# Attention on one core: sinks read as one row per partition ahead of the bias, scores issued behind the first transpositions

## The reference

```python
s = jnp.einsum('bnqhgd,bnkhd->bnhgqk', qb, kb).astype(jnp.float32) * (HEAD_B ** -0.5)
s = jnp.where(valid[None, :, None, None], s + bias[None], NEG_INF)
sink = sinks.astype(jnp.float32).reshape(1, 1, KV_HEADS, Q_PER_KV, 1)
m = jnp.maximum(s.max(-1), sink)
p = jnp.exp(s - m[..., None])
p = p / (p.sum(-1) + jnp.exp(sink - m))[..., None]
return jnp.einsum('bnhgqk,bnkhd->bnqhgd', p, vb.astype(jnp.float32))
```

## Time and profile before

| | us |
|---|---|
| median of 3 runs | 1780.65 (1779.14 to 1781.78) |
| the profiled execution, its own time | 1773.95 |
| its span, from first to last instruction | 1772.0 |
| attention stage (`at_` tiles), from the trace | 335.5 to about 467 |

### The profile page before, as it was taken

The page is one execution under the profiler, slowest core; times in us unless marked ns, Lnnn a source line. Parts: engine busy times, 40 slices in busy tenths (PEclk is TensorE's granted clock), DMA queues, the critical chain, the costliest instruction groups (busy, mean ns, idle before and its releaser), DMA issues. The chain is left out here.

```text
span 1772.0 us, 30746 instructions
## 1 busy us (share of the span) xinstructions
PE 1500.0 (85%) x12413; PEld 925.7 (52%) x12414; DVE 621.9 (35%) x1000; ACT 363.0 (20%) x797; POOL 200.3 (11%) x262
## 2 busy tenths in 40 slices
PE   7999999676787888537995799999499399999968
PEld 4666666455687777313442344444388244444433
DVE  1122460187134343562335111111578511111117
ACT  1232110166222322210001111111122111111111
POOL 3000000000222311320000101110500011111030
PEclk8999999877579989868997899999589699999988
DMA  6571120131000000014124778877601588876553
GB/s 177 145 306 59 24 48 0 28 78 25 2 4 5 5 4 4 8 70 99 36 104 155 252 275 310 288 242 247 226 1 75 178 304 288 293 249 234 183 192 130
DMA packets 138479, 237.16 MB, mean 134 GB/s; under 512 B 21570, under 2 KB 101507, under 8 KB 138090
## 3 DMA queue, kind: packets, MB, share of 16 engines
q1 hardware_dynamic: 114834, 151.01, 26.9%
q0 software_dynamic: 16912, 60.41, 9.4%
q10 hardware_dynamic: 6624, 24.12, 3.4%
HBM read 178.84 MB, written 58.21 MB: 134 GB/s over the span
## 5 line engine op out<-in xcount | busy, mean ns | idle before, releaser
L2164 PE MATMUL ex_pb<-ew_w_gate_up,ex_xT 128*128 x736 | 329.0, 600 | 6.3 <-DVE ex_xT L2209 2.7
L298 PE MATMUL pj_pb<-pj_xT,pj_w 128*128 128x348 f32 (+3 forms) x960 | 283.8, 457 | 0.4 <-ACT pj_xT L322 0.4
L298 PEld LDWEIGHTS pj_pb<-pj_xT,pj_w 128*128 128x128 f32 (+1 forms) x960 | 179.5, 187 | 102.5 <-issue 2.4
L2164 PEld LDWEIGHTS ex_pb<-ew_w_gate_up,ex_xT 128*128 128x128 f32 x736 | 137.6, 192 | 164.7 <-issue 163.8
L2147 PE MATMUL ex_pb<-ew_w_down,ex_hiddenT 128*128 x368 | 165.7, 593 | 3.4 <-ACT ex_hiddenT L2234 3.4
L2357 DVE TENSOR_TENSOR ex_hidden<-ex_hidden,ex_pb 128x256 f32<-128x256 f32 x46 | 19.4, 421 | 323.4 <-ACT ex_hidden L2229 323.4
L2147 PEld LDWEIGHTS ex_pb<-ew_w_down,ex_hiddenT 128*128 128x128 f32 x368 | 66.3, 190 | 69.9 <-issue 69.9
L1896 PE MATMUL mo_pb<-mo_w,minus_kk_then_y 128*128 128x512 f32 (+1 forms) x144 | 65.3, 607 | 21.6 <-DMA mo_w<-in_w_out 21.6
L2352 DVE COPY ex_y_rows<-ex_pb 128x512 f32<-128x512 f32 x46 | 31.8, 692 | 134.5 <-PE ex_pb L2147 134.5
L430 DVE SCALAR_TENSOR_TENSOR mixed<-pj_pb,v_mu,mixed 128x347 f32<-128x347 f32 (+3 forms) x42 | 24.0, 572 | 147.4 <-ACT mixed L372 147.3
L1896 PE MATMUL mo_pb<-mo_w,projected_qkv 128*128 128x512 f32 (+1 forms) x144 | 66.1, 614 | 9.2 <-DMA mo_w<-in_w_out 9.2
(11 more groups left out here) (429 smaller groups left out, 2187.0 us busy)
## 6 DMA issues: line engine op xcount, KB each, us to landing
ew_w_gate_up<-in_w_ex_gate SPq DMA_DIRECT2D x32, 1024.0 KB, 6.0
ew_w_gate_up<-in_w_ex_up SPq DMA_DIRECT2D x32, 1024.0 KB, 11.0
ew_w_down<-in_w_ex_down SPq DMA_DIRECT2D x32, 1024.0 KB, 13.0
scratch_slots_out<-ex_y_rows ACTq DMA_DIRECT2D x46, 512.0 KB
scratch_slots_out<-pj_tmp POOLq DMA_DIRECT2D x4, 4096.0 KB, 15.9
scratch_x_stored<-x_rows SPq DMA_DIRECT2D x16, 512.0 KB
pj_w<-in_w_in SPq DMA_DIRECT2D x7, 1024.0 KB, 8.5
minus_kk_then_y<-in_x_prompt SPq DMA_DIRECT2D x8, 512.0 KB, 5.2
```

Of the source, the lines that this page charges most:

```text
L298: last = nc.tensor.matmul(product(at)[:, 0:tn], w[:, s % NW, k, c0:c0 + mrows], xT[:, k, x0:x0 + tn], start=(k == 0), stop=(k == KD - 1))
L2164: last = mm(pb[:, 2 + u, :], xT[:, u, k, :], w[:, k, :], start=(k == 0), stop=(k == KD - 1))
```

## The change

The sinks are read by one DMA, as they lie (eight floats a partition), and it stands ahead of the eight bias loads; the samples' sinks likewise by one DMA. VectorE reads them through a rearranged view, and the semaphore counts follow. On PE, `scores(n + 2)` goes behind the transpositions of head pairs 0 and 1 of block n.

```diff
         def _(sp):
+            sp.dma_start(sinks[:, :], io["attn_sinks"].to_broadcast([P, H])).then_inc(q["sink"], 16)
             for h in range(H):
                 src = io["bias_scratch"][h, WIN - 1:WIN - 1 + P * (VW - 1)].rearrange("(p x) -> p x", x=VW - 1)[:, 0:2 * WIN]
                 sp.dma_start(bias[:, h, :], src).then_inc(q["bias_rd"], 16)
-            for v in range(KVH):
-                sp.dma_start(sinks[:, v::KVH], io["attn_sinks"][:, QPK * v:QPK * v + QPK].to_broadcast([P, QPK]),
-                             allow_slow_non_contiguous=True).then_inc(q["sink"], 16)
...
-            for v in range(KVH):
-                sp.dma_start(sinks_r[:, v::KVH], io["attn_sinks"][:, QPK * v:QPK * v + QPK].to_broadcast([R, QPK]),
-                             allow_slow_non_contiguous=True).then_inc(q["s_in"], 16)
+            sp.dma_start(sinks_r[:, :], io["attn_sinks"].to_broadcast([R, H])).then_inc(q["s_in"], 16)
...
             for n in range(NT):
+                transposes(n, 0)
+                transposes(n, 1)
                 if n + 2 < NT:
                     scores(n + 2)
-                transposes(n, 0)
-                transposes(n, 1)
...
-            dve.wait_ge(q["sink"], 32)
+            dve.wait_ge(q["sink"], 16)
...
-                link(tt(st[:, u, 0, :], st[:, u, 0, :], sinks[:, :], ALU.max))
-                tt(st[:, u, 3, :], sinks[:, :], st[:, u, 0, :], ALU.subtract)
+                by_head = lambda k: st[:, u, k, :].rearrange("p (m v) -> p m v", v=KVH)
+                of_sinks = sinks[:, :].rearrange("p (v m) -> p m v", v=KVH)
+                link(tt(by_head(0), by_head(0), of_sinks, ALU.max))
+                tt(by_head(3), of_sinks, by_head(0), ALU.subtract)
...
-                link(tt(sinks_r[:, :], sinks_r[:, :], pick[:, :], ALU.mult))
+                of_rows = sinks_r[:, :].rearrange("p (v m) -> p m v", v=KVH)
+                link(tt(of_rows, of_rows, pick[:, :].rearrange("p (m v) -> p m v", v=KVH), ALU.mult))
```

More of the change, by code:

```diff
@@ L527, in attend @@
         scr, yscr = io["sample_scratch"], io["sample_y"]
-        n_small = 16 * (4 + 2 * NS)
+        n_small = 16 * (3 + 2 * NS)
         block = m.block()
```

## The result

The changed kernel takes 1758.73 us (median of four runs, 1752.18 to 1759.59) against 1779.89 for the one before. The ratio is 0.9873, with a 95% interval of 0.9847 to 0.9899: 1.3% faster. I had forecast 1771.0 us and a range from 1766 to 1777. The sign was right and the size was not: the gain was twice as large, outside the range. What the two have in common, and where the rest is, the stages tell.

What follows compares the result with a forecast made beforehand. The prediction took the attention stage to be bound by hand-overs between engines, ScalarE, PE, ScalarE pacing most blocks. Gains of 8.5 (sinks), 0.5 (scores(1)) and 0.7 (clock) made 9.7 us: 1780.65 to 1771.0, range 1766 to 1777.

Steps and rivals of the forecast that it cites:

- The sinks: Front of the attention stage: sinks alone are late, so VectorE's first masked scores start 8.5 us earlier (7.8 to 8.6).
- The sum: Whole kernel: 8.5 + 0.5 + 0.7 = 9.7 us less, giving 1771.0 us.
- packet price: Old sinks load: 1024 packets in about 9 us, 9 ns each, one after another.
- the loads behind the sinks: SP's queue: later loads move along, first near 344.4; the rival that they don't gains 4.5 us, chance 0.09.
- the higher price: New sinks read: 128 rows of 32 B cost 1.2 us if slow, against the 0.45 us taken.
- scores(1): PE resumes before its clock falls, and VectorE's two waits vanish: gain 0 to 0.9 us, 0.5 taken.
- The cost of the order on VectorE: Masking 3.6 us late in block 0, 1.5 to 3.9 in block 5, state work hiding it elsewhere: cost nothing.
- The slower rival: Masking of blocks 2 to 7 waits for moved scores, up to 3.7 us each: 13.7 us slower, 1794; chance 0.05.
- the covers: Slack before exponentials that hides VectorE's later masking: 4.5 us in block 0, 5.3 us in block 5.
- The clock in the tails: Transpositions and products of blocks 0, 1 and 5 at a higher PE clock: 0.7 us gained, bounds 1.5 lost to 3.1 gained.
- VectorE's caps: Limit on the gain from faster tails of blocks 0 and 1: 0.9 us in block 2's exponentials, 1.6 in block 3's.
- the 2.4 less 0.9 of the working: Block 5: 0.9 us lost to scores at the low clock, up to 2.4 gained back by an upper-level tail.

Runs made afterwards that it cites:

- e6: The kernel before with the change's order on PE, and its two element-wise sinks loads put ahead of the bias loads; attention stage 126.0 us.
- e1: The changed kernel with the old order on PE, so the new sinks read alone; 1766.91 us, ratio 0.9939 to the kernel before.
- e10: The changed kernel with scores ahead of the transpositions again in blocks 0 and 5; attention stage 122.1 us.
- e7: The changed kernel with scores(4) ahead of the transpositions again in block 2 only; attention stage 118.9 us.
- e9: e1 with eight useless products filling PE's idling in block 2 alone; attention stage 119.1 us against e1's 122.4.
- e4: e1 with useless products filling PE's idling in blocks 0 to 5; 1762.75 us, ratio 0.9922, attention stage 119.0 us.
- e3: The changed kernel unaltered, run again later beside its two halves; 1761.05 us, ratio 0.9907 to the kernel before.
- e8: The changed kernel with the samples' 32 small products on PE cut in three; 1754.56 us, ratio 0.9878 to the kernel before.

## Why the forecast was too small, point by point
**The sinks: right.** The sum had VectorE starting at 342.9; it was 343.01, 8.4 us sooner for 8.5 forecast. The packet price was somewhat high: e6, with 1024 single elements ahead of the bias, starts VectorE 7.5 us after the change, some 7 ns each for the 9 of the sum; the loads behind the sinks followed (first load back at 344.08, for which I had 344.4), and no instruction waited for them. Bias is what releases VectorE now. Rows of 32 bytes cost SP one issue of 0.35 to 0.43 us; the higher price that I had weighed for them did not appear. The rearranged views left VectorE's two instructions with the sinks at 0.17 us each; the 0.02 us that I had allowed for each came from no row.

**`scores(1)`: right in kind, just above its upper end.** PE resumed at 344.49 and the product ran partly at the upper level (2.58 us for 3.78); VectorE's two waits are gone. I had taken 0.5 of 0.9; e1 shows 1.0 us (9.5 in the stage less 8.4 at the front, nothing of it in later blocks).

**The cost of the order on VectorE: right.** VectorE waits 3.29 us ahead of block 2's masking and 3.58 ahead of block 7's, where the text had about 3 and 1 to 3. ScalarE waited for the maximum in blocks 2, 3 and 7 by 0.58, 0.72 and 0.65 us, under the 1 us that I had set. In blocks 4, 5 and 6 it waited 2.69, 1.67 and 3.62 us: there the chain runs through VectorE. e10 takes VectorE's two waits away and gains nothing by it. The slower rival had its price (3.3 and 3.6 us a wait), but the covers held.

**The clock in the tails: the step that failed.** Ends of each block's exponentials on ScalarE, in us from the first DMA of the stage, and the end of the stage:

| block | 0 | 1 | 2 | 3 | 4 | 5 | 6 | 7 | end |
|---|---|---|---|---|---|---|---|---|---|
| before | 22.2 | 29.3 | 40.0 | 52.3 | 65.1 | 79.8 | 94.3 | 106.9 | 132.0 |
| e1, sinks alone | 13.8 | 19.9 | 30.6 | 42.8 | 55.7 | 70.4 | 84.8 | 97.4 | 122.4 |
| e7, change but block 2 | 13.8 | 20.3 | 30.4 | 41.9 | 54.8 | 69.5 | 83.9 | 94.7 | 118.9 |
| e9, e1 with filler in block 2 | 13.8 | 19.9 | 30.6 | 42.9 | 53.0 | 68.5 | 82.9 | 94.5 | 119.1 |
| e4, e1 with filler in blocks 0 to 5 | 13.7 | 19.8 | 28.6 | 39.4 | 50.4 | 66.7 | 79.3 | 94.2 | 119.0 |
| the change | 13.8 | 19.9 | 29.5 | 41.0 | 54.0 | 65.9 | 80.3 | 91.4 | 115.8 |

Between e1 and the change it is 1.1 us at block 2 and 1.8 at block 3; I had written 0.9 and 1.6 as VectorE's caps. Block 7 adds 1.5, just the 2.4 less 0.9 of the working. What is missing altogether is the 2.8 us more at block 5 (1.7 becomes 4.5).

The prediction has a gain for the tails of blocks 0 and 1 and for that of block 5; for the tail of block 2 it has no term, and gives no reason why not. It also takes VectorE's cap at blocks 2 and 3 as a cap for all that follows. In e1 PE idles 3.91 us ahead of the second transpositions of block 2. In the change `scores(4)`, 2.00 us of work, stands in that pause and 1.74 us are left; the clock stayed up, and the tail took 3.3 us instead of 5.9. It also began 1.8 us sooner, by the gain in blocks 0 and 1 that was in my own sum. Behind it on PE are the samples' scores, for which VectorE had waited 7.82 us; now it doesn't wait, and copies them 51.5 us after the first DMA of the stage, in e1 55.9. These 4.5 us are the 1.8 and the 2.7 of the tail together. In the trace of before, VectorE's copy of those scores:

```profile
400.87 0.19 DVE L858 COPY at_s_scoresT<-at_pb 128x32 f32<-128x32 f32 x1 [7.82 <-PE at_pb L648]
```

The copy frees VectorE's state update and with it the masking of block 5, whose exponentials are 4.5 us sooner too. There VectorE had no slack: ScalarE's 0.89 us said so, and I read that only as a cap on what block 4 could win. e7 takes this step out of the change and loses 2.7 us by it at block 5 (its 3.1 us of stage include the delay ahead of the edit); e9 keeps PE at work there in e1 and gains 1.9 us at block 5 and 3.3 in the stage. The last 0.6 us, behind block 7, I have not traced.

So the step that failed is the term for the clock in the tails: 0.7 taken, 3.1 as the bound, 6.6 measured (115.8 against 122.4). The mechanism was right, the size was not, because the tail of block 2 and what hangs on it had been put at nothing. The forecast stage of near 122 us is what e1, without the new order, has. That it is the clock is shown for block 2 by e7 and e9, and for the blocks up to 6 by e4, which moves nothing and gains as much. That block 5's 1.5 us is the clock too is read from its tail alone (products 1.53 us for 2.54). Added up anew, 8.4 + 1.0 + 6.6 = 16.0 us, for 16.1 in the profile.

**The rest of the first difference: scatter, as far as the runs show.** The medians of the first comparison lie 21.2 us apart, those of e3's series 15.2. The stages behind the attention are the same code in all kernels, and in the thirteen profiles the recurrence took 240.2 to 247.0 us and all that follows it 1059.2 to 1066.3, in no order that goes with the edits. The stage's 16.1 us are 0.91%, inside e3's interval and just outside that of the first comparison. That the surplus there is this scatter is argued from these spreads, not shown. Medians alone would have had me look for 5 us that the edited stage does not hold.

## What to carry to other kernels
A load that names single elements cost by the element here and held up what was issued behind it on the queue (e6): read such a vector in the order in which it lies, and rearrange in the view of the instruction that uses it. When work is moved on PE, ask not only who waits for it but where the pause goes: in this kernel 2.93 us of pause ahead of the first transpositions of block 2 and 1.74 ahead of the second left the clock up, while 3.67 or 3.91 us ahead of the second were followed by half the clock for the whole tail. And when a gain is given to some blocks, say of each other block why it has none: here the tail of block 2 was left out, and was worth 2.7 us.

## What the runs showed that I had not expected
A wait of 3.3 us of VectorE, through which the chain runs, can be worth having: e10 removes it, and that of 3.6 us in block 7's masking, and loses 6.3 us, of which up to 0.5 stood ahead of its edit. Eight useless products in one block (e9) shorten the stage by 3.3 us. The Trainium skill (TensorE: Matmul & The Clock Gate, Part 1) says that activity releases the throttled state; e9 agrees, with the clock at 1.00 in place of 0.50 in the same tail. The level that PE gets at a given place is partly chance: the same `scores(1)` took 2.58 to 3.11 us, and `scores(4)` ran at the upper level in one kernel (the change, 2.00 us) and at the lower in another with the same code up to there (e8, 3.79 us). Even so, two profiles of the changed kernel, taken in different series, differ by 0.06 us in the length of the stage.
